# Sums of weighted w_ada rows: scaling on ScalarE with accumulating DMAs from GpSimd, in place of two GpSimd operations a piece

## What is computed

```python
c_act = jax.nn.silu(c)
mod = c_act @ w_ada[l] + b_ada[l]                 # (1, 2048) @ (2048, 12288)
sh1, sc1, gt1, sh2, sc2, gt2 = jnp.split(mod, 6, axis=-1)
h = modulate(rms_norm(x, g_mix[l]), sh1, sc1)
z = h @ w_in[l]
...                                               # two attentions, gates
x = x + gt1[:, None, :] * (merged @ w_out[l])
h = modulate(rms_norm(x, g_ffn[l]), sh2, sc2)
...                                               # convolution, gated FFN
x = x + gt2[:, None, :] * y
```

## Time and profile before

| | |
|---|---|
| time, median of 3 runs | 3091.49 us (3090.83 to 3091.84) |
| span of the profiled execution | 3088.4 us |
| TensorE busy with matmuls | 2772.0 us (90%) |
| VectorE busy | 2006.4 us (65%) |
| ScalarE busy | 1288.5 us (42%) |
| GpSimd busy | 1037.5 us (34%) |
| mean granted TensorE clock | 0.960 of full speed |
| DMA | 585.40 MB, mean 190 GB/s |

### The profile page before, as it was taken

One profiled execution on the slowest core, in us unless ns is written; L12 is line 12 of the kernel. 1 busy time (PEld: TensorE's weight loads), 2 busy tenths in 40 slices (PEclk: granted clock), 3 DMA queues, 4 the chain that ended last, 5 costly groups with the idle time before them and its releaser, 6 DMA issues. The chain is left out here.

```text
span 3088.4 us, 35464 instructions
## 1 busy us (share of the span) xinstructions
PE 2772.0 (90%) x12279; PEld 2258.1 (73%) x12279; DVE 2006.4 (65%) x1808; ACT 1288.5 (42%) x1505; POOL 1037.5 (34%) x538
## 2 busy tenths in 40 slices
PE   0599899989988799999999959998898999999998
PEld 0477787667767678888788748777587888888886
DVE  7776566887975777677766674456655555555554
ACT  1223455334433444444444434444245444444443
POOL 0598454858945433222322250002200111111111
PEclk9989899989999899999999979998999999999999
DMA  9666554746664665655666515454054555555553
GB/s 392 240 205 230 198 206 175 245 144 210 242 234 164 236 204 190 204 195 191 198 204 207 187 55 187 153 177 150 1 164 152 190 190 190 190 191 190 189 190 122
DMA packets 266919, 585.40 MB, mean 190 GB/s; under 512 B 14300, under 2 KB 16676, under 8 KB 263900
## 3 DMA queue, kind: packets, MB, share of 16 engines
q1 hardware_dynamic: 266844, 584.41, 56.1%
HBM read 582.26 MB, written 2.11 MB: 189 GB/s over the span
## 5 line engine op out<-in xcount | busy, mean ns | idle before, releaser
L1206 DVE TENSOR_TENSOR sb_wlo<-sb_raw,sb_whi 128x1024 fp32r<-128x1024 f32 x896 | 1322.9, 1487 | 883.4 <-ACT sb_whi L818 882.5
L818 ACT ACTIVATE sb_whi<-sb_raw 128x1024 fp32r<-128x1024 f32 x896 | 945.2, 1059 | 1452.8 <-PE lin L393 1250.8
L391 PE MATMUL lin<-sb_whi,sb_act_hi 128*128 128x512 f32 x2880 | 1154.9, 401 | 89.7 <-DVE sb_wlo L1206 46.4
L393 PE MATMUL lin<-sb_whi,sb_act_lo 128*128 128x512 f32 x2880 | 1136.2, 395 | 0.0
L392 PE MATMUL lin<-sb_wlo,sb_act_hi 128*128 128x512 f32 x2880 | 1136.0, 394 | 0.0
L391 PEld LDWEIGHTS lin<-sb_whi,sb_act_hi 128*128 128x128 f32 x2880 | 550.7, 191 | 218.9 <-issue 53.2
L393 PEld LDWEIGHTS lin<-sb_whi,sb_act_lo 128*128 128x128 f32 x2880 | 549.6, 191 | 117.9
L392 PEld LDWEIGHTS lin<-sb_wlo,sb_act_hi 128*128 128x128 f32 x2880 | 551.3, 191 | 111.8 <-issue 0.2
L1758 POOL TENSOR_TENSOR sb_ada_in<-sb_ada_in,sb_small 128x1024 f32<-128x1024 f32 x128 | 301.0, 2351 | 293.5 <-DMA sb_ada_in<-in_w_ada_dram 174.7
L1760 POOL TENSOR_TENSOR sb_ada_acc<-sb_ada_acc,sb_ada_in 128x1024 f32<-128x1024 f32 x128 | 383.4, 2995 | 10.0
L391 PE MATMUL lin<-sb_whi,sb_hid_hi 128*128 128x512 f32 x704 | 278.4, 395 | 6.3 <-DVE sb_hid_lo L1487 3.7
(11 more groups left out here) (292 smaller groups left out, 1770.5 us busy)
## 6 DMA issues: line engine op xcount, KB each, us to landing
sb_raw<-in_w_in_dram SPq DMA_DIRECT2D x88, 1024.0 KB, 5.9
sb_raw<-in_ffn_w_gu_dram SPq DMA_DIRECT2D x88, 1024.0 KB, 5.1
sb_ada_in<-in_w_ada_dram SPq DMA_DIRECT2D x128, 512.0 KB, 3.9
sb_raw<-in_gla_w_in_dram SPq DMA_DIRECT2D x48, 1024.0 KB, 5.2
sb_raw<-in_w_gate_dram SPq DMA_DIRECT2D x44, 1024.0 KB, 5.3
sb_raw<-in_w_up_dram SPq DMA_DIRECT2D x44, 1024.0 KB, 5.2
sb_raw<-in_w_down_dram SPq DMA_DIRECT2D x44, 1024.0 KB, 5.1
sb_raw<-in_ffn_w_down_dram SPq DMA_DIRECT2D x44, 1024.0 KB, 5.0
```

Of the source, the lines that this page charges most:

```text
L391: pe.matmul(o, x_hi[:, kt + q, t], whi[:, w], start=first and q == 0, stop=False)
L393: m = pe.matmul(o, x_lo[:, kt + q, t], whi[:, w], start=False, stop=last and q == 1)
L818: act.activation(whi[:, idx % RING * HALF:(idx % RING + 1) * HALF], raw[:, idx // 2 % RING, idx % 2 * HALF:(idx % 2 + 1) * HALF], ACT.Copy ...
L1206: dve.tensor_tensor(wlo[:, c], raw[:, idx // 2 % RING, idx % 2 * HALF:(idx % 2 + 1) * HALF], whi[:, c].bitcast(fp32), ALU.subtract).then_i ...
```

## The change

The number of chunks, their buffers and the queue that loads them stay. What is done to a chunk, and where, is new:

- Chunks 0 to 107: ScalarE scales the chunk in place (`ada_scale`) and GpSimd then issues a DMA from `ada_in` to the sum, in SBUF, with the operation add (`ada_add`). The first two chunks of a piece are copied by such a DMA, so the sum is not cleared. sc2 gets a sum of its own, `ada_first`, in the place of the token buffer.
- Chunks 108 to 127 (the ten rounds of F1): VectorE multiplies and adds in one operation (`ada_last`), at halves 21 and 23 of each round.
- A table, `CHUNKS_AT`, puts each chunk behind a slab, on all engines alike: chunk n behind slab 4 + n up to 63 (so one behind every slab of A from the fifth, of B, and of the first 12 of C1), 64 to 95 behind the slabs of C2 and O, and the rest in U and F1p.
- `ada_columns(0)` moves from the end of A to the end of B, and `ada_columns(1)` from the end of C1 to its half 11 of the second iteration. The wait of TensorE for sc2 ahead of B goes.
- The 16 small loads of the bias table move from between A and B to behind the first slab of C1's second iteration, and SyncE no longer waits there for the write of the table.
- Several loops over iterations are written out on the engines, since the table is indexed by constants.

```diff
+ADA_PIECES = (4, 3, 2, 5)
+CHUNKS_AT = {}
+for _n in range(108):
+    _at = 4 + _n if _n < 64 else 8 + _n if _n < 96 else 20 + _n if _n < 102 else (124, 125, 126, 126, 127, 127)[_n - 102]
+    CHUNKS_AT.setdefault(_at, []).append(_n)
...
             sp.dma_start(raw[:, s % RING, :].rearrange("p (k n) -> p k n", k=4), src).then_inc(slab_in[s % RING], 16)
-
-        def ada_chunk(n, piece, j):
-
-            if not (isinstance(n, int) and n < 2):
-                sp.wait_ge(ada_left, n - 1)
+            for n in chunks_after(phase, it, per, s):
+                ada_chunk(n)
+
+        def ada_chunk(n, kt=None, half=None):
+
+            if kt is None:
+                kt, half = n % 32 // 2, n % 2
+                if n > 1:
+                    sp.wait_ge(ada_done[half], 8 * (n - half))
+            else:
+                sp.wait_ge(ada_done[half], 16 * 54)
+                sp.wait_ge(ada_late[half], kt - 5)
...
+        def hankels():
+
+            sp.wait_ge(sem("e_out"), 16)
+            sp.wait_ge(sem("ada_T"), 1)
+            for h in range(NH):
...
+        for it in range(2):
+            cols_body(it, "C1", C_GATE, hankels if it else None)
...
-        pe.wait_ge(sem("mod_made"), 1)
         def b_body(it):
...
         pe.wait_ge(sem("sb_out"), NH)
+        ada_columns(0)
...
+                if (it, idx) == (1, 11):
+                    pe.wait_ge(sem("mod_made"), 1)
+                    ada_columns(1)
...
+        def ada_scale(n):
+
+            kt, half = n % 32 // 2, n % 2
+            act.wait_ge(ada_come[half], 8 * (n - half) + 16)
+            act.activation(ada_in[:, half, :], ada_in[:, half, :], ACT.Copy, scale=cact[:, kt:kt + 1]).then_inc(sem("ada_mul"), 1)
+
         def body(it, phase, per, hooks, upto=None, start=RING):
 
             for idx in range(start, per + RING if upto is None else upto):
                 split(it, phase, per, idx)
                 for step in hooks.get(idx, ()):
                     step()
+                if idx % 2:
+                    for n in chunks_after(phase, it, per, idx // 2):
+                        ada_scale(n)
...
+        def ada_last(it, half):
+
+            c = slice(half * (D // 2), (half + 1) * (D // 2))
+            dve.wait_ge(ada_come[half], 8 * (2 * it + 108) + 16)
+            dve.wait_ge(ada_done[half], 16 * 54)
+            dve.wait_ge(ada_late[half], it + 1)
+            dve.scalar_tensor_tensor(ada_acc[:, c], ada_in[:, half, :], cact[:, ds(6 + it, 1)], ada_acc[:, c], ALU.mult, ALU.add).then_inc(ada_late[half], 1)
...
+                if n == 0 and phase == name:
+                    for half in range(2):
+                        add(21 + 2 * half, lambda half=half: ada_last(it, half))
...
-            pool.wait_ge(ada_come[half], 8 * (n - half) + 16)
-            pool.wait_ge(sem("ada_sum"), n)
-            pool.tensor_tensor(ada_in[:, half, :], ada_in[:, half, :], col.to_broadcast([P, D // 2]), ALU.mult).then_inc(sem("ada_mul"), 1)
             pool.wait_ge(sem("ada_mul"), n + 1)
-            pool.tensor_tensor(ada_acc[:, c], ada_acc[:, c], ada_in[:, half, :], ALU.add).then_inc(sem("ada_sum"), 1)
...
+            if first and n >= 64:
+                pool.wait_ge(sem("ada_T"), n // 32)
+            if not first:
+                pool.wait_ge(ada_done[half], 8 * (n - half))
+            pool.dma_start(acc[:, c], ada_in[:, half, :], accum_op=ALU.bypass if first else ALU.add).then_inc(ada_done[half], 16)
...
         for g in range(4):
             pool.wait_ge(free0, 2 + G0["U"] + g + 1)
             combine(y1, g, 0, g == 3)
-            if g < 3:
-                for k in ((), (0, 1), (2, 3))[g]:
-                    pairs_of(96 + 2 * k, k, 48 + k)
+            for s in ((), (), range(12, 16), range(16, 18))[g]:
+                chunks("U", s)
```

More of the change, by code:

```diff
@@ L265, in _, with cols_body @@
         sp.dma_start(relb[:], A["rel_bias"]).then_inc(sem("rel_in"), 16)
-        def a_body(it):
+        def cols_body(it, phase, col0, after=None):
             for s in range(8):
[L269 to L282, removed]
+                slab(it, phase, 16, s, w_in[:, 4 * (s % 4):4 * (s % 4) + 4, it * 2 * NB + col0 + s // 4 * NB:it * 2 * NB + col0 + s // 4 * NB + NB])
@@ L941, in sb_act @@
             return hooks
-        with act.Fori(0, 3) as it:
+        for it in range(0, 3):
             body(it, "B", 16, drains2(it, "B", lambda k: dsz[:, 0, cols(it, k)], sb_act(it)))
@@ L963, in ix_act @@
             return hooks
-        with act.Fori(0, 2) as it:
+        for it in range(0, 2):
             body(it, "C1", 16, drains2(it, "C1", lambda k: gate_sb[:, 0, cols(it, k)], ix_act(it)))
@@ L1280, in _ @@
         dve.wait_ge(sem("gs_made"), 1)
+        for late in ada_late:
+            dve.nop().then_inc(late, 1)
         dve.nop().then_inc(free1, 1)
@@ L1361, in ix_dve @@
             return {4 * u + 6: [lambda u=u: add(u)] for u in range(4)}
-        with dve.Fori(0, 2) as it:
+        for it in range(2):
             body(it, "C1", 16, drains2(it, "C1", lambda k: gate_sb[:, 1, cols(it, k)], ix_dve(it)))
@@ L1793, in _ @@
         sb_stage(1, 1)
[L1794 to L1805 removed]
+        for s in range(1, 32):
+            chunks("B", s)
+            h = s // 4 + 2
+            if s % 4 == 3 and h < NH:
+                pool.wait_ge(sem("sb_o"), h - 1)
+                sb_stage(h, h % 2)
+        chunks("C1", 0)
         def ix_stage(p, u):
```

180 lines of the change are left out of this document (74 added, 106 removed).

## The result

The changed kernel takes 3143.74 us (median of 4, 3139.12 to 3151.87), the kernel before 3091.4 on the same chip: ratio 1.0175, 95% interval 1.016 to 1.019. It is 52 us slower where 74 us faster was forecast. The profiled execution has a span of 3141.9 us.

A forecast was written before the change was run, and what follows sets the result against it. TensorE's idle time and lost clock from 112 to 1081 us, some 190 us, partly from GpSimd slowing VectorE, were taken as the bound. Gains 96 less 18 (DMA) less 4 (late chunks) gave 74: 3017.5 us; 8 in 10: 2992 to 3085.

The forecast's parts named there:

- The gains: All stages: time won back from TensorE's idle time and lost clock, 96 us before the DMA's loss and late chunks.
- up to the end of A: Start of A: 8 us ahead of the first matmul, 11 of later idle time, 5 of clock, together 24 us gained.
- the gap after A: Between A and B: with the small loads moved, 18.4 us shrinks to about 5; 13 and 4 of clock, 17 gained.
- C1: Stage C1: late `wlo` halves hold nearly all idle time and lost clock; 19 us less 2 for small loads, 17 gained.
- U and F1p: Stages U and F1p: the chain of drains, norm and features stays but for slowed VectorE steps; 5 and 4 us gained.
- late chunks: In U: chunks that come late cost 4 us.
- the small loads: In C1, ahead of its tenth slab: 7.8 us of issue, about 8 of reserve left; 2 us charged, bare 8.
- the rival in which VectorE stays slow: GpSimd, issuing DMAs, also works on SBUF, so only the moved loads and perhaps 5 us count: 3070 us; chance 0.07.
- The DMA's own price: A to O: an add moves its bytes twice, 6.3 us a slab; loss 31 us, 18 after the ring's reserve.
- the rival in which the engines fill up: DMA engines: bytes twice at 332 GB/s, 7.9 us a slab, 3155 us; full engines 0.22, of which 0.10 slower.
- the chain: Scaling, issue, DMA, slab landing, split: 16.5 us per three slabs; over 8.6 for issue and DMA, 3035 to 3060; chance 0.06.
- The signs that I listed: `wlo` at 1.2 us, GpSimd under 400, gap near 5, TensorE idle half or less of 123, 172 to 301 growing at most 10.

The follow-up runs named there:

- narrow adds: Changed kernel, but each accumulating DMA that adds covers 32 of 1024 columns, the other sums left out; all waits and queues stay: 3004.49 us, ratio to before 0.9724.
- vec: Changed kernel, but VectorE multiplies and adds all 108 chunks in one fused operation each, without ScalarE's scaling or adding DMAs: 2988.93 us, ratio to before 0.9676.
- vec_load2: vec plus 52 accumulating DMAs in A and B, two in flight, from the constants into two spare sums: 3019.23 us, ratio to before 0.9768.
- deep2: Changed kernel with four buffers in place of two for chunks 0 to 51, two adds in flight: 3081.62 us, ratio to before 0.9978.
- single: Kernel with narrow adds, but in A and B SyncE asks for a chunk only when the add before is done: 3097.37 us, ratio to before 1.0018.
- hank: Kernel before, with only the 16 small loads moved into C1, behind its ninth slab: 3080.13 us, ratio to before 0.9962.
- vec_spread: vec, but chunks 96 to 107 come one to a slab in U and none in F1p: 2982.58 us, ratio to before 0.9652.
- deep: Changed kernel with four buffers for chunks 0 to 51, but GpSimd waits for each add before the next: 3244.94 us, ratio to before 1.0495.

## Why the prediction was wrong, point by point

**The gains were right in sum, less so by stage.** They stood at 96 us, less 4 for late chunks. Before to narrow adds is 84 us by the medians of one group (3088.52 less 3004.49) and 86 by the profiled spans. By stage, in profiled time: up to the end of A 30.0 (24 forecast), B, where the gap after A lies, 20.1 (17 and part of 3), C1 7.6 (17), C2 11.8 (10), O 12.9 (16), U and F1p 12.9 (9, with the 4 for late chunks 5), F1 8.9 lost (0). That the sum comes so near is in part luck: 9 too high in C1 and 9 in F1 meet 6 too low at the start and 8 in U and F1p. C1 was too high; in vec it gains 13.0, so that a part of the shortfall is the scaling on ScalarE or the loop, even with narrow adds. In the changed kernel the small loads cost more there than the 2 us charged: TensorE has a gap of 10.0 us at 618. The first slab behind them is asked for at 616.40, and its split begins at 626.30. The loads alone do not make this gap: with narrow adds it is 1.6 us and in vec there is none, with the same loads at the same place. U and F1p were too low. F1's loss is that of the late chunks, below. That GpSimd's operations slowed VectorE, and that its DMA issues do not, is shown: with the products and sums gone, the median `wlo` half takes 1.23 us and the mean up to F1 1.25, and the 39 halves that run beside a DMA issue and nothing else of GpSimd's take 1.23 at most. GpSimd's remaining copies and additions still slow a half, to 2.31 us at most. So the rival in which VectorE stays slow did not come about. GpSimd's busy time is 391.7 us, under the 400 of the list.

**The DMA's own price was right too.** I took the add as twice its bytes and 6.3 us for a slab. The packets take 323 against 162 ns; where only the engines bind, a slab takes 6.3 to 6.4 us (vec_load2 and deep2, once the reserve of the ring is used up). The 7.9 us of the rival in which the engines fill up did not come about. Of my loss from it, 18 in all with O, the part in A and B measures 8 in deep2 and 30 at most, in vec_load2.

**The step that failed is the chain.** I checked one path: scaling, issue, DMA, a slab's landing, its split, once in three slabs, 16.5 us, with 8.6 us for issue and DMA. I did not check the loop of the buffers: a chunk's load stands in it as well, and it has to close in two slabs, 11.0 us at TensorE's 5.5. Its terms by the changed kernel are 3.9 + 1.6 + 8.7 = 14.2. My own rows show the form of the loop, but not that it binds: a slab of twice the size landed in 5.8 us, so some 3 to 4 for the chunk, with 1.06 for the scaling and the DMA at 1.3 to 2.5 us of bare engine time that is at most 8. What was missing was that a DMA's latency is not its engine time. It took 7.0 to 7.5 us from issue to landing (median) where the engines were busy with it for 2.6.

Both parts are needed, the loop and the line in front of the engines. One whole add of A, with the loop not yet at its limit, was issued at 191.71, and SyncE asked for the next chunk of its buffer at 196.25, 4.5 us on; no whole add of this kernel landed sooner. With 4.5 in place of 8.7 the loop would be 10.0 us, 5.0 a slab, and would close in time (an estimate from these rows). Why there is a line while the engines could move more is argued, not tested: held by the adds, SyncE asks in bursts, a chunk and a slab at 236.15 and again at 238.61, then nothing until 250.36. The path that I did check was over its limit as well. Issue and DMA took 8.7 us against my 8.6, and a slab's landing 8.9 (median) where I had 5.8: from one add at 241.63 to the add three chunks on, at 260.79, it is 19.2 us, 6.4 a slab. The loop, at 7.1, is the longer of the two. I gave the chain 0.06 and 3035 to 3060, as "a few gaps"; it is a tax on every slab that has a chunk.

The Trainium skill, page "DMA: Bandwidth & Descriptors", section "Anatomy of one DMA — SWDGE (gpsimd) path", gives such a DMA a fixed cost of 2.0 us, most of it for its completion. The narrow add agrees, 2.0 to 2.1 us from issue to landing in single. With the page's rate the whole piece would be at 3.2 us, an estimate by that page; the least that a whole add took is 4.5, so the measured 2.6 us of engine time fit better, and the rest of the 7.0 to 7.5, some 2.5 to 3 us, is the line in front of it. The narrow add's own median in A, 5.2 us beside slabs against 2.1 without a line, gives the same 3.

**Where the 138 us went** (narrow adds to the changed kernel, profiled time by stage): up to the end of A 14.3, B 55.9, C1 11.6, C2 9.7, O 20.4, U 6.8, F1p 13.3, F1 6.1. Of the 70.2 up to the end of B the four buffers give back 62. B is hit hardest because its slabs carry attention steps: ScalarE works in order, waits for a chunk or a slab, and the step behind it is late. TensorE's waits there for two attention tiles are 20.6 and 15.0 us, where the narrow adds leave 3.2 and none:

```profile
PE aux L514 <- DVE sb_lk L1354: 20.6, 7, 5.4
PE aux L508 <- ACT sb_qk_sb L935: 15.0, 5, 4.1
```

TensorE idles 51.3 us and is granted a clock of 0.90 in B (0.98 with narrow adds), and its busy time for the same matmuls grows from 200.6 to 215.2 us: the idle stretches cost again in the clock. The 68 us from C1 on were not separated: deep2 leaves two buffers there and its stages are as in the changed kernel. That it is the same loop is argued, not shown.

**The gap after A.** I forecast some 5 us; it is 14.9 in the changed kernel, 8.3 in hank, 5.8 in vec, 10.7 in deep2. Moving the small loads did its part; then SyncE stood behind an add there as well. The copies into `kdup` come behind the splits of B's first two slabs, and these began at 287.33 and 294.39, each as soon as its slab had landed; A's last matmul ended at 285.55.

**Late chunks.** I charged 4 us and named U. They cost at the start of F1: in F1p's last two slabs SyncE can ask for no chunk before the two before it are summed, and the first slabs of F1 stand behind. vec to vec_spread, 7.7 us of F1, is the price there with the shortest loop.

**The signs that I listed.** `wlo` at 1.2: yes. GpSimd under 400: yes. Gap near 5: no. Idle time at half or less of 123 us: no, it grew; 11.8 + 51.3 + 14.1 + 14.5 + 18.9 + 16.6 in A to U is 127 us, and with the 26.9 of F1p, which the 123 include, 154. The stretch from A's fifth slab to its end, 129 us before, within some 10 us: no, 140.6, and that is 11.7 more. ScalarE waiting for slabs with the DMA share near 1, as a sign of full engines: both appeared, and the reading was wrong. Share 1.00 with 292 GB/s was less than the same engines moved with four buffers, 323 at 1.05.

## What to carry to other kernels

A buffer that is loaded, worked on and sent on by a DMA closes a loop: add up load, operation, issue and the DMA's latency from issue until the one who waits sees it, divide by the number of buffers, and compare with the pace of the work; the engine time of the DMA is not the number for this. A DMA share of 1.0 does not show that the DMA engines are the limit; the landing time of the next transfer (8.9 against 18.7 us here) and the rate do. And before a sum is moved to DMAs, try it as one fused operation on the engine whose contention is being removed: here that is 100 us faster than before in vec and 108 in vec_spread, with 1.28 us a piece.

## What the runs showed of the hardware

- An accumulating DMA from SBUF to SBUF takes its engines 323 ns for a packet of 4 KB, a copying one 162. Its latency was 2.0 to 2.1 us for 32 columns with no line at the engines (single). For 1024 columns it was 4.5 at the least, 7.0 to 7.5 with slabs beside it (medians, changed kernel), and 9.4 to 9.6 where one add followed the other (deep).
- GpSimd's issue of one such DMA takes 0.87 us, and a `wlo` half on VectorE at the same time keeps its 1.23 us. Beside GpSimd's products and sums it took up to 3.43.
- ScalarE's in-place scaling of 128x1024 takes 1.15 us, where its copy of the same shape takes 1.06; VectorE's fused multiply and add of it 1.28 us.
- The 16 engines moved 323 GB/s at a share of 1.05 with adds in the mix (deep2). With them full, single issues of a slab on SyncE's queue lasted up to 3.0 us in place of 0.45.
